# Gate stage of a retrieval mixer: rounds of weighted sums begin three batches later, two of them run behind the last batch, and the first value blocks wait for the last round of their own place

## What is computed

```python
experts = ...            # 128 expert numbers for each token, out of 16384
gates = softmax(top_s)   # one weight for each of them
u = expert_u[es]
vv = expert_v[es]
a = gelu(einsum('tkd,td->tk', u, xs))
y = einsum('tk,tkd->td', gs * a, vv)
```

## Time and profile before

| | |
|---|---|
| median of 3 executions | 1862.25 us (1861.77 to 1866.41) |
| time of the profiled execution | 1859.29 us |
| its span | 1857.5 us |
| TensorE busy | 1766.8 us (95%) |
| VectorE busy | 1267.7 us (68%) |
| GpSimd busy | 903.7 us (49%) |
| ScalarE busy | 298.4 us (16%) |
| gate stage: first batch to first value block, on TensorE | 1262.04 to 1375.37 us |

### The profile page before, as it was taken

The page is one execution under the profiler, slowest core; times in us unless marked ns, Lnnn a source line. Parts: engine busy times, 40 slices in busy tenths (PEclk is TensorE's granted clock), DMA queues, the critical chain, the costliest instruction groups (busy, mean ns, idle before and its releaser), DMA issues.

```text
span 1857.5 us, 20549 instructions
## 1 busy us (share of the span) xinstructions
PE 1766.8 (95%) x7508; PEld 1103.8 (59%) x7508; DVE 1267.7 (68%) x2592; ACT 298.4 (16%) x689; POOL 903.7 (49%) x818
## 2 busy tenths in 40 slices
PE   5987999998999999999999999999899999999996
PEld 3675844554444458678888888886554434444442
DVE  1212568989579799989999888869855323336767
ACT  0120012555000001111100100116630000000000
POOL 1000336656456323356675666567765554435541
PEclk9998999998999999999999999999999999999998
DMA  9997769888999968779999999999999999999995
GB/s 395 394 362 301 287 197 395 313 316 308 384 339 406 397 241 324 249 263 409 395 409 405 409 397 408 399 398 355 361 363 410 409 343 409 409 410 409 409 410 234
DMA packets 171205, 670.16 MB, mean 361 GB/s; under 512 B 19770, under 2 KB 20922, under 8 KB 166364
## 3 DMA queue, kind: packets, MB, share of 16 engines
q0 software_dynamic: 112368, 409.74, 57.8%
q1 hardware_dynamic: 53984, 243.29, 33.5%
q10 hardware_dynamic: 4752, 15.81, 2.2%
HBM read 659.27 MB, written 7.39 MB: 359 GB/s over the span
## 4 chain that ended last, share of the span: by engine, by line
PE 43%; DVE 24%; DMA 17%; POOL 8%; issue 6%; ACT 1%; SPq 1%; DVEq 0%; ACTq 0%; POOLq 0%
PE psum L1057 18%; DMA arena<-in_expert_u_dram,arena 8%; POOL arena L641 8%; DVE psum L1991 7%; DMA arena<-in_expert_v_dram,arena 6%; DVE arena L1700 5%; PE psum L840 3%; PE psum L829 3%; PE psum L1010 2%; PE psum L815 2%; PE psum L1081 2%; PE psum L1084 2%; PE psum L1118 2%; PE psum L1178 2%; PE psum L826 1%
## 5 line engine op out<-in xcount | busy, mean ns | idle before, releaser
L641 POOL DMA_INDIRECT arena<-in_expert_u_dram,arena x384 | 484.2, 1261 | 314.1 <-DVE arena L1700 187.3
L641 POOL DMA_INDIRECT arena<-in_expert_v_dram,arena x384 | 384.4, 1001 | 365.5 <-DVE psum L1991 187.0
L1700 DVE CUSTOM_DVE_ANT_0 arena<-arena 128x1024 f32<-128x1024 f32 x384 | 458.5, 1222 | 137.4 <-DMA arena<-in_expert_u_dram,arena 136.1
L1991 DVE SCALAR_TENSOR_TENSOR psum<-arena,psum 128x1024 f32<-128x1024 f32 x254 | 327.1, 1288 | 198.0 <-DMA arena<-in_expert_v_dram,arena 183.9
L1057 PE MATMUL psum<-arena 128*128 128x512 f32 x1024 | 442.9, 594 | 0.8 <-DMA arena<-in_expert_v_dram 0.8
L983 PE MATMUL psum<-arena 128*128 128x256 f32 x2048 | 442.7, 379 | 0.0
L983 PEld LDWEIGHTS psum<-arena 128*128 128x128 f32 x2048 | 389.2, 190 | 52.3
L1057 PEld LDWEIGHTS psum<-arena 128*128 128x128 f32 x1024 | 193.7, 190 | 250.1 <-issue 249.9
L1478 ACT ACTIVATE arena<-psum 128x512 f32<-128x512 f32 x64 | 38.2, 597 | 373.2 <-PE psum L983 373.2
L840 PE MATMUL psum<-arena 128*128 128x512 f32 x192 | 86.9, 605 | 0.8 <-ACT arena L1264 0.8
L1155 PE MATMUL psum<-arena 128*128 128x384 f32 x256 | 85.2, 486 | 0.0
(11 more groups left out here) (201 smaller groups left out, 1490.2 us busy)
## 6 DMA issues: line engine op xcount, KB each, us to landing
arena<-in_expert_uT_dram SPq DMA_DIRECT2D x128, 512.0 KB, 6.8
arena<-in_expert_v_dram SPq DMA_DIRECT2D x128, 512.0 KB, 6.8
arena<-in_w_ada_dram SPq DMA_DIRECT2D x12, 2048.0 KB, 13.7
arena<-in_w_in_dram SPq DMA_DIRECT2D x11, 2048.0 KB, 12.4
arena<-in_w_query_dram SPq DMA_DIRECT2D x8, 2048.0 KB, 11.3
arena<-in_w_in_dram SPq DMA_DIRECT2D x30, 512.0 KB, 8.4
arena<-in_w_o_dram SPq DMA_DIRECT2D x16, 512.0 KB, 6.7
arena<-in_expert_u_dram,arena POOLq DMA_INDIRECT x384, 9.8
```

What stands on the lines that cost most here:

```text
L641: pool.indirect_dma_start(slot, None, table[0], bass.IndirectOffsetOnAxis(ap=number, axis=0)).then_inc(land, 16)
L1700: dve.tensor_tensor_reduce(row, row, U2B[e], 1.0, 0.0, ALU.mult, ALU.add, DOTS[e % 2][:, k:k + 1]).then_inc(u_free, 1)
L1991: dve.scalar_tensor_tensor(ys, row, weight, ys, ALU.mult, ALU.add).then_inc(v_free, 1)
```

## The change

Two things are changed. The rounds are placed by a new function: none lies behind the batches 0 to 3, round 0 lies behind batch 4 (it was batch 1), the 18 rounds 0 to 17 are spread evenly up to batch 30, and rounds 18 and 19 both come behind batch 31, the last. ScalarE's copies of the weights are moved alike. And the value loads 129, 130 and 131 each wait for the last round of their own place: 129 and 130 for round 18, 131 for round 19.

```diff
@@ SyncE, the stream of blocks
-                if n == NKEYS + 1:
-                    sp.wait_ge(summed, GATE_ROUNDS)
+                if NKEYS < n < NKEYS + RING:
+                    sp.wait_ge(summed, LAST_SUM[GROUP + n - NKEYS - 1] + 1)
@@ TensorE
             for i in range(BATCHES):
                 place(i)
-                for r in range(i * GATE_ROUNDS // BATCHES, (i + 1) * GATE_ROUNDS // BATCHES):
+                for r in range(rounds_ahead(i), rounds_ahead(i + 1)):
                     sum_round(r)
+            for r in range(rounds_ahead(BATCHES), GATE_ROUNDS):
+                sum_round(r)
@@ ScalarE
             for i in range(BATCHES):
-                for r in range(i * GATE_ROUNDS // BATCHES, (i + 1) * GATE_ROUNDS // BATCHES):
+                for r in range(rounds_ahead(i), rounds_ahead(i + 1)):
                     columns(r)
                 if i:
                     gate_hot(i)
+            for r in range(rounds_ahead(BATCHES), GATE_ROUNDS):
+                columns(r)
@@ new
+def rounds_ahead(i):
+
+    return max(0, (i - 3) * GATE_ROUNDS // (BATCHES - 1))
```

## The result

| | before | changed |
|---|---|---|
| median | 1862.25 us (7 executions, 1857.69 to 1869.17) | 1872.88 us (7 executions, 1863.9 to 1880.16) |
| ratio | | 1.0054, 95% interval 1.0032 to 1.0075 |
| profiled execution, its span | 1859.29 us, 1857.5 us | 1880.16 us, 1878.4 us |

What follows compares the result with a forecast made beforehand. The prediction took GpSimd's issue of 80 rows without a pause to bound the gate stage. Its terms, 9.6 - 1.8 + 1.0 - 0.8 = +8.0 us, put on the median of 1862.25, gave 1870 us, range 1864 to 1875.

Steps and rivals of the forecast that it cites:

- Round 0 later: Gate stage: row 11 needs round 0's place, so GpSimd stands still until round 0 behind batch 4 ends; +9.6 us.
- No further rows wait: Gate stage behind row 11: rows 15 and 19 find their rounds done, GpSimd paces again; no further time added.
- Meetings avoided: Gate stage: three L2047 of VectorE pass while GpSimd stands, with no row to lengthen; -1.8 us.
- sum of +6.0: Gate stage: alternative total if L2046 also blocks GpSimd, so three of them are saved too, 3 x 0.68 us.
- Loads beside the last rows: End of gate stage: loads 129 and 130 go while the last rows are under way, delaying row 79; +1.0 us.
- Load 128 covered: Start of value blocks: the last two rounds cover load 128, so the wait of 0.77 us goes; -0.8 us.
- Passed on whole: From first value block to the end: the gate stage's delay of 8.0 us reaches the kernel's end in full.
- second rival: Behind the gate stage: earlier loads and unused DMA time absorb part of the delay; 1863.4 to 1867.7 us, chance 0.16.
- GpSimd catches up: Gate stage after row 11: rows fall between the L2047 and come faster; -1.8 us, 1860.5 us, chance 0.08.
- The transfers are the limit: Gate stage: full DMA engines, not GpSimd, set the pace, so lost time stays lost; +11.4 us, 1873.7 us, chance 0.11.

Runs made afterwards that it cites:

- e2: Changed kernel with the old wait of the value loads (load 129 waits for all 20 rounds); 1.0059 of the kernel before.
- e4: Changed kernel with rounds still starting behind batch 4, but round 19 alone behind batch 31; new load waits kept; 1.0054 of the kernel before.
- e6: Kernel before, with L2047 reading the numbers 0 to 127 from psum instead of SBUF; 0.9957 of the kernel before.
- e9: e2 with load 128 waiting for round 19 as well, so no value load goes beside the last rows; 1.0082 of the kernel before.
- e1: Kernel before with only the new waits of value loads 129 to 131, rounds where they were; 0.9995 of the kernel before.
- e11: Kernel before with only round 0 moved, behind batch 2 instead of batch 1; 0.9996 of the kernel before.
- e5: Kernel before with L2047 left out from batch 2 on, an instruction of 8 columns in its place (wrong gates); 0.9939 of the kernel before.
- e12: e7 with rounds as early as they can be, from behind batch 0, and load 128 after batch 30; 0.9933 of the kernel before, median 1851.7 us.
- e7: Changed kernel with the edit of e6 (numbers of L2047 in psum); 1.0014 of the kernel before.
- e8: e6 with round 0 behind batch 0, load 128 after batch 30 and the load waits of e1; 0.9965 of the kernel before.
- e10: Kernel before with 8 places for rows instead of 11, the ring buffers not lent to rows; 1.0143 of the kernel before.
- e3: Changed kernel with round 0 behind batch 1, rounds 0 to 17 spread over all 32 batches, 18 and 19 behind the last; 1.0018 of the kernel before.

## Why the prediction was right, and where it was not

The direction, the place and about the size were right: 1870 forecast, 1872.88 measured, +8.0 forecast against some +10. By its steps, against the traces (before and changed in the table), of which each is one execution:

1. *Round 0 later, +9.6.* Measured 26.52 - 17.76 = +8.8, and 10.1 and 8.7 in e2 and e4. The mechanism is right, and e4 shows that it is enough by itself. That the size fits so well in this execution is in part luck: the first two batches ran 1.4 us longer at the lower clock, and the first batch started 9.43 us behind row 0 instead of 11.77. Measured from the first batch, round 0 ends 11.1 us later than before, where the sum had 9.6. The sum also said that VectorE ran without a pause up to the fifth L2047; it had waited 1.91 us for the first batch, and this wait became 3.67.
2. *No further rows wait.* Right but for row 79, 0.69 us; TensorE's waits for rows are back from round 4 on (1.05 us).
3. *Meetings avoided, -1.8.* This step failed. The 69 rows took 0.1 us less. Before, 27 rows were lengthened by 14.4 us together, in the changed kernel 25 by 13.9: the 26 L2047 that were left go with 0.54 us of it each, L2046's share included, where the 29 before went with 0.50, so that three fewer saved 0.5 us and not 1.8, and the wait of row 79, 0.69 instead of 0.30, took 0.4 back. My three examples, 2.0 us together, were all of the kind that lengthens a row; 5 of the 29 before and 4 of the 26 now lengthen none, and how much the others cost hangs on where the rows fall. The sum of +6.0 fails in the same way: that L2046 holds GpSimd was right (e6), but I had charged each instruction as if it always met a row at its very start.
4. *Loads beside the last rows, +1.0.* The landing grew by 3.2 us, so the term was mis-sized. The loads are half of it at most: e9, without any beside the rows, still has 2.0 of it. The rest is likely that rows issued faster at the end land later on full DMA engines, which I had not seen; this stays open.
5. *Load 128 covered, -0.8.* Right, the value block doesn't wait. But the sum lacked a term: round 19, after 4.6 us of waiting, ran at 1.2 GHz and took 3.64 us instead of 1.92, +1.7. Together "to value" grew by 0.9.

8.8 - 0.1 + 3.2 + 0.9 is 12.8 us in this execution, against the 10 us of the medians and the 8.0 of the sum; two terms of the wrong size and one left out, all on the slow side, less the 0.8 of step 1, hold the difference of 4.8. So the forecast of 8.0 lies nearer to the medians than its terms deserve.

*Passed on whole:* right, by the last column of the table; the second rival (the rest takes it up) is out. *GpSimd catches up:* out, 99.4 to 100.1 us for the 69 rows in the kernel before, the changed one, e1, e2, e4 and e11; only the one execution of e9, in the changed order, made up 3.6 us of the 9.7 by which its row 11 was late. *The transfers are the limit:* out for the stage as it was, by e5 and e6; once VectorE no longer holds GpSimd, a stretch runs at 405 GB/s, near what the engines carry elsewhere.

The first reading of the waits (TensorE waits 10 us for rows, so ask later) was the trap. e12 does the opposite of the change, asks as early as can be, and with the numbers in psum is the fastest.

## What to carry to other kernels

Before moving a consumer back because it waits, look at whether its producer ever pauses: if it doesn't, the waits are the producer's pace, and a later consumer only frees the producer's buffers later. The first use of each buffer was the sensitive one here: all that the change lost to the stop was lost there, three batches late, while one batch late couldn't be told from none (e11). The gain lay in the producer's pace, one operand moved from SBUF to psum, and the changed order didn't pay with it either (e7). Whether an earlier order pays isn't shown: e12 gained 0.24% over e6, within the intervals, and e8 nothing.

## What the runs showed of the hardware that I had not expected

- A float32 two-input instruction of VectorE on 128x1024 takes 1.22 us with both inputs in SBUF and with one of them in psum; only in the first case are GpSimd's indirect DMA instructions that start inside it lengthened (27 of 69 rows by 0.53 us in the mean before; in e6 6 of 69, by L2046, which kept two SBUF inputs). The instruction of VectorE itself isn't lengthened when it starts while a row is under way.
- A short wait of TensorE often cost twice. In the changed kernel the last round followed a wait of 4.57 us and ran at a granted clock of 0.50, 1.2 GHz, 3.64 us instead of 1.92. In e1, e2, e7, e9, e10 and e11 it took 3.0 to 3.6 us behind waits of 2.3 to 4.8 us. The last rounds of the kernel before, behind 1.83 us, and of e4, behind 1.51, took 1.92. The length of the last wait doesn't decide it alone: the last round of e3 took 3.33 us behind 1.38, after a round that had waited 5.52 and taken 3.64, and single rounds of e9 and e10 kept 1.92 and 1.93 behind 2.29 and 2.20.
- Three places of 11 taken away cost 27 us (e10), more than the 4.7 us by which row 11 started later: in its profiled execution the rows from row 11 on took 17 us more.
